# Waits for both scaled identities placed ahead of the four products of a combination

## The reference

```python
u = expert_u[ec]
act = jax.nn.gelu(jnp.einsum('cd,ced->ce', xc, u).astype(jnp.float32))
return jnp.einsum('ce,ced->cd', gc * act, expert_v[ec])
```

## Time and profile before

| what | value |
|---|---|
| median of 3 runs | 1396.33 us (1395.01 to 1400.92) |
| profiled execution | 1396.65 us |
| its span | 1394.7 us, so 1.95 us lie around it |
| mean granted TensorE clock | 0.929 |
| TensorE matmul busy | 1143.0 us (82%) |
| VectorE, ScalarE, GpSimd busy | 776.3, 491.6, 274.7 us |
| HBM read | 376.12 MB, of which the gathers 268.45 MB |

### The profile page before, as it was taken

How to read it: one execution, slowest core, us unless ns; L and a number is a source line. 1 busy time by engine, 2 the same in 40 slices (tenths; PEclk the granted TensorE clock), 3 DMA queues, 4 the chain that set the end, 5 groups by cost and what they waited for, 6 DMA issues and landing times.

```text
span 1394.7 us, 15234 instructions
## 1 busy us (share of the span) xinstructions
PE 1143.0 (82%) x5688; PEld 668.7 (48%) x5688; DVE 776.3 (56%) x1875; ACT 491.6 (35%) x1300; POOL 274.7 (20%) x261
## 2 busy tenths in 40 slices
PE   6989995887786677668886666679988998999997
PEld 2877672432242223112221111134866887899883
DVE  5475656887846998465454444430466657732111
ACT  1121222544433344345333333321686543113101
POOL 0000002434343444444443333200000000000000
PEclk9987976989999999989999999899998999999999
DMA  9995506989999999999999999914422131114130
GB/s 391 322 378 194 196 1 261 335 339 390 408 420 421 421 407 385 422 421 422 421 421 422 421 421 422 411 66 181 182 84 98 61 122 61 63 62 180 61 121 30
DMA packets 56949, 378.16 MB, mean 271 GB/s; under 512 B 7171, under 2 KB 10412, under 8 KB 11820
## 3 DMA queue, kind: packets, MB, share of 16 engines
q0 software_dynamic: 36864, 268.45, 47.2%
q1 hardware_dynamic: 19344, 106.71, 20.2%
q10 hardware_dynamic: 668, 2.04, 0.4%
HBM read 376.12 MB, written 1.06 MB: 270 GB/s over the span
## 4 chain that ended last, share of the span: by engine, by line
PE 47%; DMA 23%; DVE 18%; ACT 7%; issue 3%; POOL 1%; ACTq 0%; SPq 0%; POOLq 0%; DVEq 0%
DMA AR<-in_puv,idx 20%; PE ps L591 19%; PE ps L895 7%; PE ps L599 7%; DVE AR L1622 6%; PE ps L1063 3%; PE ps L813 2%; DMA W<-in_w_mod 2%; DVE AR L1741 1%; PE ps L841 1%; ACT L2248 1%; DVE hT L1315 1%; ACT acc L2059 1%; DMA X<-in_x 1%; PE ps L760 1%
## 5 line engine op out<-in xcount | busy, mean ns | idle before, releaser
L895 PE MATMUL ps<-AR,acc 128*64 128x512 f32 x912 | 348.8, 670 | 169.0 <-ACT acc L2059 166.9
L2459 POOL DMA_INDIRECT AR<-in_puv,idx x256 | 274.4, 1072 | 624.1 <-PE ps L895 368.8
L591 PE MATMUL ps<-hT,W 128*128 128x256 f32 x1216 | 284.6, 392 | 11.6 <-DVE AR L1346 6.1
L895 PEld LDWEIGHTS ps<-AR,acc 128*64 128x64 f32 x912 | 81.6, 144 | 410.9 <-ACT acc L2059 330.7
L591 PEld LDWEIGHTS ps<-hT,W 128*128 128x128 f32 x1216 | 237.4, 198 | 50.8 <-DVE AR L1346 6.9
L1622 DVE CUSTOM_DVE_ANT_0 AR<-AR,mixT 128x1024 f32<-128x1024 f32 x128 | 156.6, 1225 | 150.3 <-DMA AR<-in_puv,idx 150.3
L1622 DVE CUSTOM_DVE_ANT_0 AR<-AR,tok 128x1024 f32<-128x1024 f32 x128 | 153.6, 1219 | 63.6 <-DMA AR<-in_puv,idx 63.6
L2174 ACT ACTIVATE av<-av 128x1 f32<-128x1 f32 x256 | 51.4, 201 | 305.5 <-DVE av L1622 305.2
L2059 ACT ACTIVATE acc<-fold,av 128x64 f32<-128x64 f32 x228 | 79.3, 348 | 7.4
L2176 ACT ACTIVATE av<-av,gwp 128x1 f32<-128x1 f32 x256 | 75.4, 294 | 8.3
L599 PE MATMUL ps<-W,hT 128*128 128x512 f32 (+3 forms) x224 | 67.7, 460 | 0.0
(11 more groups left out here) (350 smaller groups left out, 1326.8 us busy)
## 6 DMA issues: line engine op xcount, KB each, us to landing
W<-in_w_in SPq DMA_DIRECT2D x50, 1024.0 KB, 7.1
W<-in_w_mod SPq DMA_DIRECT2D x24, 1024.0 KB, 14.6
W<-in_w_out SPq DMA_DIRECT2D x4, 1024.0 KB, 6.0
W<-in_wq SPq DMA_DIRECT2D x4, 1024.0 KB
AR<-in_puv,idx POOLq DMA_INDIRECT x256
W<-in_wba SPq DMA_DIRECT2D x4, 1024.0 KB
W<-in_wbb SPq DMA_DIRECT2D x4, 1024.0 KB
W<-in_wo SPq DMA_DIRECT2D x4, 1024.0 KB, 5.9
```

The source lines that it names most:

```text
L591: t = mm(b[:, o:o + S], slab(i)[:, k, c:c + P], src[:, k, :], start=(k == 0), stop=(k == 7))
L895: t = mm(of(("E", a, c))[64 * g:64 * g + 64, :], dg_at((2 * p + g) % NDG, late), GB[:, places[g], D + c * 512:D + c * 512 + 512], start=(m ...
L2459: eng.indirect_dma_start(GB[:, n, :], None, puv, bass.IndirectOffsetOnAxis(ap=idx[:, a, c:c + 1], axis=0)).then_inc(*gp.dma(f"g{n}", "gat" ...
```

## The change

In `combine` on TensorE one wait for both identities (and for both accumulators' old users) stands ahead of all four products, and the waits inside the loops are gone. Order, number and operands of the products stay.

```diff
--- before.py
+++ after.py
@@ -889,9 +889,9 @@
             def combine(p, places, late):
                 a, m = p // 64, p % 64
                 olds = [take(("E", a, c))[1] for c in range(2)] if m == 0 else ([], [])
+                pe.wait_ge(*olds[0], *olds[1], ("dg", p, 0), ("dg", p, 1))
                 for c in range(2):
                     for g in range(2):
-                        pe.wait_ge(*olds[c], ("dg", p, g))
                         t = mm(of(("E", a, c))[64 * g:64 * g + 64, :], dg_at((2 * p + g) % NDG, late),
                                GB[:, places[g], D + c * 512:D + c * 512 + 512], start=(m == 0), stop=(m == 63))
                         if c == 1:
```

## The result

| | median, us | range, us |
|---|---|---|
| the kernel before | 1395.67 | 1394.71 to 1400.92 |
| with the change | 1416.50 | 1414.50 to 1422.32 |

The ratio is 1.0148, 95% interval 1.0108 to 1.0189: about 21 us slower. The forecast was 1398.7 with a range to 1404.5, so the result lies outside it, on the side of the rival that had 0.13. The profiled execution took 1414.5 us, span 1412.7, and its mean TensorE clock was 0.863 where it had been 0.929.

What follows compares the result with a forecast made beforehand. After 545 us DMA transfers were taken to bound the loop, with dry DMA before 330 and VectorE pacing 440 to 545. Profiled 1396.65 + 2.4 = 1399.05, set against a median 0.3 lower: 1398.7 us, range 1394.3 to 1404.5.

Steps and rivals of the forecast that it cites:

- The end of the four products stays: TensorE's combination: with the first product started later, the last product ends 0.00 to 0.01 us later, taken as 0.
- The late release, three early fetches, 2.4 us: Before 330 us, three fetches waiting for group 0's buffer start 0.78, 0.83 and 0.78 us later, 2.4 us in all.
- The pairs from 545 us on cost nothing: Some 73 late pairs: 5.5 us of DMA queue hides the 0.83 us later release, even 2.6 at the low clock.
- the end of the loop: Last combination after the final gather: unchanged at 1.93 us, taken as 0; at the low clock 1.75 us longer.
- The clock before 545 us: TensorE's clock in the early loop: nothing in the forecast sum; a lower clock there was left to rival 3.
- rival 3: Bunched work leaves TensorE at low clock more often, 215 to 400 us; five slow combinations give 1407.4 us; chance 0.13.
- VectorE's stretch, 440 to 545 us, taken as 0: Where VectorE's chain sets the pace, late fetches cost 0, with 1.6 us as the bound above.
- rival 4: TensorE passes can't overtake, so four products need 0.48 us more; 5.8 us on top, 1404.5 us; chance 0.02.
- Low clock at every burst: Skill's rule that DMA waits between short TensorE bursts return the low clock every burst; trace agreed partly, mean 0.94.

Runs made afterwards that it cites:

- e7: Kernel before with one more, already met wait per pair (group 1's identity waited for twice ahead of its first product): 1395.31 against 1397.41 us, ratio 0.9974.
- e6: The change for pairs 56 to 127 alone, earlier pairs waiting as in the kernel before: ratio 1.0022 to the kernel before.
- e9: The changed kernel run once more, unedited, in a later series: ratio 1.0144 to the kernel before.
- e4: Kernel before with loops exchanged, both products of group 0 behind its identity, then both of group 1: 1393.16 us, ratio 0.9982; later 1391.02, 0.9974.
- e8: Kernel before with a zero product added after group 0's first product, ahead of the wait for group 1's identity: ratio 1.0047.

## Why the prediction was wrong

- *The end of the four products stays*: right at the high clock, 1.94 us for eight passes behind the second identity. Two small errors: the number of waits did not stay at two instructions (128 more), and the start is 0.14 us behind the identity instead of 0.05. By e7 it costs nothing to be seen.
- *The late release, three early fetches, 2.4 us*: right in size. Alone it measured 0.24%, some 3 us (0.7 to 6.1). Its profile is 2.2 us late at fetch 33, behind the three fetches, but goes on to 6.3 at fetch 65, so the places are not settled.
- *The pairs from 545 us on cost nothing*: right. e6 has 0.22%, an interval that holds 0; in its profile the last combination, at the low clock, takes 3.56 us for 1.93, and that 1.63 is the end of the loop that the forecast put at 0, with 1.75 as its bound.
- *The clock before 545 us*: here the forecast failed. Its sum held nothing for it, and rival 3 got 0.13, with the words that "the first product often ran with other work close around it, so that a gap closed by 1.07 us matters little". The clock there shows otherwise: from 245 to 405 us its mean is 0.81 in the change and 0.82 in e9, for 0.90 before. I had computed TensorE's gap, 3.04 us in one piece, and used it for the steady stretch alone, where a low clock is harmless.
- *The price of rival 3*: its place was right (215 to 400 us), its size was not: 8.7 us beyond the release, where 12 to 17 were measured. It counted 1.74 us for each of five combinations and nothing for the projections and attention between them, which slow down with the clock and stand on the same chain: 1.4 us at one step of line 841, 0.7 for eight passes of 773, 0.6 at 735.
- *VectorE's stretch, 440 to 545 us, taken as 0*: about right. Between fetches 77 and 113, which start at 444.33 and 542.19 before, the change loses 0.1 and 2.8 us in its two profiles, at a clock of 0.76; the forecast's bound was 1.6.
- *Program order* (rival 4): no sign of it in any run. By the rule of the Trainium skill that it stood for ("TensorE: Matmul & The Clock Gate", section "Part 3: Packing small matmuls — row/col tiling"), e4 should have been slower with both identities ready; its 1.94 us disagree. So the sentence ahead of the prediction that an engine's instructions start in the order written doesn't hold for passes on the two halves: two run at 648.49, though the first four in the program are all of group 0, and such four by themselves take 1.93 us.
- *Low clock at every burst*: the mean behind 556 us fell from 0.95 to 0.80, but long and short combinations take turns (3.61 and 1.94 us). What the section "HAM oscillation — how this bites in real kernels" of the same page of the Trainium skill says of short bursts between waits holds in direction, not for every burst.

## What to carry to other kernels

Work that runs early in a gap on TensorE can be worth more than its own length: taken out of the gap, it may move the granted clock and lengthen all that follows. When an edit only shifts matmuls behind a later wait, price the clock for the stretch in which TensorE is on the chain, and for all of TensorE's work there, not only for the matmuls that move. The order that put more useful work into the gap, all products of the operand that comes first, was here no slower than the kernel before, at the highest clock of all runs (0.946, as in e8).

## What the runs showed that was not expected

- Useless work made a kernel faster: the change took 1403.63 us with a zero product per pair and 1416.50 without, each in its own series (ratios 1.0058 and 1.0148 to the kernel before).
- The clock followed the length of work in the gap by degrees: 0.870, 0.905 and 0.931 with none, 256 and 512 columns.
- Two waits in a row made an instruction more and moved a start by 0.09 us; one more wait in the kernel before had the same delay and no cost that could be seen.
- Two products of group 0 ahead of both of group 1 take no longer than four in turns, 1.94 us.
